# The opening of a decoder-layer kernel: x first, the modulation of feature block 0 alone, and four idle-fill products

## The reference, cut to what matters

```
mod = silu(c) @ w_ada + b_ada          # w_ada 1024 x 6144; six rows of 1024: sh1 sc1 gt1 sh2 sc2 gt2
h   = rms_norm(x, g_norm_mix) * (1 + sc1) + sh1
proj = h @ w_in                        # columns: q f i g | attention q k v | merge gates
```

## Time and profile before

| what | value |
|---|---|
| median of three runs | 951.63 us |
| profiled execution | 952.29 us |
| its span, first to last instruction | 950.6 us |
| TensorE busy | 915.2 us (96%) |
| VectorE, ScalarE, GpSimd busy | 441.2, 363.2, 439.2 us |
| mean granted TensorE clock, of full | 0.995 |
| HBM read | 111.76 MB |

### The profile page before, as it was taken

One profiled execution on the slowest core, in us unless ns is written; L12 is line 12 of the kernel. 1 busy time (PEld: TensorE's weight loads), 2 busy tenths in 40 slices (PEclk: granted clock), 3 DMA queues, 4 the chain that ended last, 5 costly groups with the idle time before them and its releaser, 6 DMA issues.

```text
span 950.6 us, 11767 instructions
## 1 busy us (share of the span) xinstructions
PE 915.2 (96%) x4487; PEld 771.1 (81%) x4487; DVE 441.2 (46%) x707; ACT 363.2 (38%) x482; POOL 439.2 (46%) x390
## 2 busy tenths in 40 slices
PE   2999999998999999999999999999999999999996
PEld 1788888987888888888888888888888888888885
DVE  4843467765456979976723526232222222200005
ACT  4433425242344223453323326555444544412113
POOL 2588433443243344345544445644544445444554
PEclk9999999999999999999999999999999999999998
DMA  9832221212143758443435131322223322233212
GB/s 316 264 132 89 89 89 45 89 45 89 45 142 132 225 175 287 147 133 123 189 104 214 60 132 45 128 95 88 88 88 99 120 89 88 88 122 100 89 44 89
DMA packets 93767, 114.47 MB, mean 120 GB/s; under 512 B 2158, under 2 KB 84250, under 8 KB 93726
## 3 DMA queue, kind: packets, MB, share of 16 engines
q1 hardware_dynamic: 93726, 113.89, 36.1%
HBM read 111.76 MB, written 2.12 MB: 120 GB/s over the span
## 4 chain that ended last, share of the span: by engine, by line
PE 44%; issue 30%; POOL 19%; DVE 3%; ACT 1%; DMA 1%; POOLq 0%; SPq 0%; DVEq 0%; ACTq 0%
PE bank L1051 44%; POOL w_lo L656 18%; DVE bank L1514 1%; DMA x_in<-in_x_dram 1%; DVE bank L1988 0%; DVE x L1989 0%; PE bank L1054 0%; DVE xn_ffn L1885 0%; ACT h_tmp L762 0%; POOL masks L593 0%; ACT w_hi L735 0%; POOL masks L630 0%; DVE h_tmp2a L1570 0%; DVE part L1516 0%; DVE bank L1512 0%
## 5 line engine op out<-in xcount | busy, mean ns | idle before, releaser
L656 POOL TENSOR_TENSOR w_lo<-w_raw,w_hi 128x512 fp32r<-128x512 f32 x292 | 387.3, 1357 | 457.5 <-ACT w_hi L735 452.5
L1051 PE MATMUL bank<-h_hi,w_hi 128*128 128x512 f32 (+1 forms) x880 | 340.3, 390 | 0.1
L1051 PE MATMUL bank<-h_lo,w_hi 128*128 128x512 f32 (+1 forms) x880 | 336.7, 386 | 0.0
L1051 PE MATMUL bank<-h_hi,w_lo 128*128 128x512 f32 (+1 forms) x880 | 261.1, 385 | 0.0
L735 ACT ACTIVATE w_hi<-w_raw 128x2048 fp32r<-128x2048 f32 x72 | 137.5, 1910 | 223.2 <-PE bank L1051 223.2
L1051 PEld LDWEIGHTS bank<-h_hi,w_lo 128*128 128x128 f32 x880 | 165.6, 188 | 33.2
L1051 PEld LDWEIGHTS bank<-h_lo,w_hi 128*128 128x128 f32 x880 | 165.4, 188 | 32.8
L1051 PEld LDWEIGHTS bank<-h_hi,w_hi 128*128 128x128 f32 x880 | 165.1, 188 | 32.8 <-POOL h_lo L643 0.3
L1051 PE MATMUL bank<-w_hi,act_hi 128*128 128x512 f32 x176 | 68.5, 389 | 0.0
L1051 PE MATMUL bank<-w_lo,act_hi 128*128 128x512 f32 x176 | 68.5, 389 | 0.0
L1051 PE MATMUL bank<-w_hi,act_lo 128*128 128x512 f32 x176 | 68.5, 389 | 0.0
(11 more groups left out here) (250 smaller groups left out, 1133.6 us busy)
## 6 DMA issues: line engine op xcount, KB each, us to landing
w_raw<-in_w_in_dram SPq DMA_DIRECT2D x32, 1024.0 KB, 5.2
w_raw<-in_w_up_dram SPq DMA_DIRECT2D x22, 1024.0 KB, 5.0
ada<-in_w_ada_dram SPq DMA_DIRECT2D x16, 1024.0 KB, 5.3
w_raw<-in_w_down_dram SPq DMA_DIRECT2D x11, 1024.0 KB, 4.8
ada<-in_w_ada_dram SPq DMA_DIRECT2D x16, 512.0 KB, 8.4
w_raw<-in_w_out_dram SPq DMA_DIRECT2D x4, 1024.0 KB, 5.1
x_in<-in_x_dram SPq DMA_DIRECT2D x4, 512.0 KB, 5.4
w_raw<-in_w_in_dram SPq DMA_DIRECT2D x8, 256.0 KB, 7.2
```

The source lines that it names most:

```text
L656: ins = pool.tensor_tensor(wlo[slot][:, cols], raw[slot][:, cols], whi[slot][:, cols].bitcast(F32), ALU.subtract)
L1051: return pe.matmul(o, lhsT, rhs, start=start, stop=stop, **kw)
```

## The change

The four feature pairs become five groups, `MOD_GROUPS`: block 0 alone, block 1 alone, then pairs. A single block's modulation is a sum over 256 columns, two products with ones, and so on. The loads of w_ada come in quarters of the 1024 rows, two DMAs each (128 columns of shift and of scale per row for a single block, 256 for a pair), so there are 40 issues in place of 16; the shares of pair 0 follow the first group and the other shares follow the groups of pairs 1 to 3. The seven loads of small rows are issued by ScalarE at its start.

Each tile of x gets its own inverse root on GpSimd; VectorE scales tiles 0 to 2 and ScalarE tile 3. TensorE first transposes the small rows, then block 0 and 1 of each tile as it comes, with a product of 512 columns that nothing reads behind each of tiles 0, 1 and 2 (`full_rate`: the identity with the normed x, into a bank that unit 0 later starts anew), and one of 256 columns behind the first modulation. VectorE makes a group's sums and then its `modulated`, in strict turn. All low parts of h but those of blocks 6 and 7 are GpSimd's, now ahead of the shares. ScalarE makes h of a pair ahead of its shares' conversion, and a unit's share waits for its own load alone. TensorE runs a pair's products by pass over both units: high with high, the next blocks' transposes, high with low h, the next modulation, low weights. SyncE's unit 2 waits for the third group's modulation, and VectorE's conversion of it for the fourth's and the last shares' high parts. The remaining hunks rename semaphore counts.

```diff
+MOD_GROUPS = ((0,), (1,), (2, 3), (4, 5), (6, 7))
...
+        def group_columns(g):
+            k0, n = MOD_GROUPS[g][0], len(MOD_GROUPS[g]) * P
+            return ada[k0 // 2][:, :, 256 * (k0 % 2):256 * (k0 % 2) + 2 * n]
...
+            def ada_quarter(g, q):
+                ks = slice(2 * q, 2 * q + 2)
+                k0, n = MOD_GROUPS[g][0], len(MOD_GROUPS[g]) * P
+                for i in range(2):
+                    sp.dma_start(group_columns(g)[:, ks, n * i:n * i + n],
+                                 cols_of(w_ada, D * i + P * k0, n)[:, ks, :]).then_inc(ada_in[g][q], 16)
+            def first_shares(j):
+                for u in range(2):
+                    sp.dma_start(raw[u][:, 512 * j:512 * j + 512].rearrange("p (k c) -> p k c", c=256),
...
+            for g in range(len(MOD_GROUPS)):
+                for q in range(4):
+                    ada_quarter(g, q)
+                if g != 1:
+                    first_shares(max(g - 1, 0))
+            ready(sp, ("mod1", 2))
             sp.dma_start(raw[2][:, :].rearrange("p (k c) -> p k c", c=256), unit_source(2)).then_inc(raw_in[0], 16)
...
-            pool.wait_ge(sq_done, TT)
-            inverse_root(0, TT)
+            for t in range(TT):
+                pool.wait_ge(sq_done, t + 1)
+                link(pool.tensor_scalar(rstd[:, t:t + 1], ssq[:, t:t + 1], 1.0 / D, EPS, ALU.mult, ALU.add))
+                pool.tensor_tensor(rstd[:, t:t + 1], rstd[:, t:t + 1], mhalf[:, 0:1], ALU.pow).then_inc(first_root, 1)
...
             for j in range(KT // 2):
+                if j < KT // 2 - 1:
+                    low_h(2 * j)
+                    if j:
+                        low_h(2 * j + 1)
                 low_share(j, 0)
                 low_share(j, 1)
-                if 0 < j < KT // 2 - 1:
-                    low_h(2 * j)
-                if j < KT // 2 - 1:
-                    low_h(2 * j + 1)
+                if j == 0:
+                    low_h(1)
...
+            def rows(dst, r0, src, n):
+                act.dma_start(dst[r0:r0 + n, :], src).then_inc(vec_in, 16)
+            rows(vec_rows, B_ADA, b_ada.rearrange("l (k p) -> (l k) p", p=P), 48)
...
             def high_share(j, u):
                 cols = slice(512 * j, 512 * j + 512)
+                act.wait_ge(share_in[j][u], 16)
...
-            act.wait_ge(rstd_done, 1)
-            for t in range(TT - 1):
-                act.activation(xn_in[:, t, :], x_in[:, t, :], ACT.Copy, scale=rstd[:, t:t + 1]).then_inc(xn_done[0], 1)
+            t = TT - 1
+            act.wait_ge(first_root, TT)
+            act.activation(xn_in[:, t, :], x_in[:, t, :], ACT.Copy, scale=rstd[:, t:t + 1]).then_inc(xn_done[t], 1)
             for j in range(KT // 2):
-                act.wait_ge(share_in[j], 16 * 2)
-                high_share(j, 0)
+                if j == 0:
+                    high_share(j, 0)
+                first_h(2 * j)
+                if j:
+                    first_h(2 * j + 1)
+                    high_share(j, 0)
                 high_share(j, 1)
-                first_h(j)
                 if j == 0:
+                    first_h(1)
                     act.wait_ge(lbd_done, 1)
...
+            def first_modulation(g):
+                b = claim(pe, ("mod1", g))
+                pe.wait_ge(pair_done, g + 1)
+                for t in range(2 * len(MOD_GROUPS[g])):
+                    ins = mm(b[:, t:t + 1], part[:, g % 2, t * P:(t + 1) * P], ones[:, 0:1])
+                filled(ins, ("mod1", g))
+            def full_rate(t, n):
+                mm(bank[BANKS["g", 0, 0][0]][:, 0:n], ident[:, :], xn_in[:, t, 0:n])
             def transposed_x(k):
                 b = claim(pe, ("xT", 0, k))
-                if k == 0:
-                    pe.wait_ge(xn_done[0], TT - 1)
-                    pe.wait_ge(xn_done[1], 1)
                 for t in range(TT):
                     ins = transpose(b[:, t * P:(t + 1) * P], xn_in[:, t, k * P:(k + 1) * P])
                 filled(ins, ("xT", 0, k))
+            def first_transposes():
+                bb = [claim(pe, ("xT", 0, k)) for k in range(2)]
+                for t in range(TT):
+                    pe.wait_ge(xn_done[t], 1)
+                    for k in range(2):
+                        ins = transpose(bb[k][:, t * P:(t + 1) * P], xn_in[:, t, k * P:(k + 1) * P])
+                        if t == TT - 1:
+                            filled(ins, ("xT", 0, k))
+                    if t < TT - 1:
+                        full_rate(t, S)
...
+            def growing_products(u, k, w, a):
+                j = k // 2
+                hi, lo = (s[u][:, :].rearrange("p (k c) -> p k c", c=256) for s in (whi, wlo))
+                if w is wlo:
+                    if j < KT // 2 - 1:
+                        pe.wait_ge(lo_share, 2 * j + u + 1)
+                    else:
+                        pe.wait_ge(lo_done, u + 1)
+                elif a is h_lo:
+                    pe.wait_ge(h_lo_done[k], 1)
                 else:
                     pe.wait_ge(h_hi_done, k + 1)
+                    if j < KT // 2 - 1:
+                        pe.wait_ge(hi_share, 2 * j + u + 1)
+                    else:
+                        pe.wait_ge(hi_done, u + 1)
...
+            high, h_low, w_low = (whi, h_hi), (whi, h_lo), (wlo, h_hi)
+            vector_rows()
+            first_transposes()
+            first_modulation(0)
+            full_rate(3, 256)
+            for u in range(2):
+                growing_products(u, 0, *high)
+            first_modulation(1)
+            for u in range(2):
+                growing_products(u, 0, *h_low)
+            for u in range(2):
+                growing_products(u, 0, *w_low)
+            for u in range(2):
+                growing_products(u, 1, *high)
+            for k in (2, 3):
                 transposed_x(k)
-            vector_rows()
-            for j in range(KT // 2):
-                first_modulation(j)
-                if j:
-                    growing_products(j - 1, 1)
-                if j < KT // 2 - 1:
-                    for k in (2 * j + 2, 2 * j + 3):
-                        transposed_x(k)
-                growing_products(j, 0)
-            growing_products(KT // 2 - 1, 1)
+            for what in (h_low, w_low):
+                for u in range(2):
+                    growing_products(u, 1, *what)
+            first_modulation(2)
+            for g in (2, 3):
+                for k in MOD_GROUPS[g]:
+                    for u in range(2):
+                        growing_products(u, k, *high)
+                for k in MOD_GROUPS[g + 1]:
+                    transposed_x(k)
+                for k in MOD_GROUPS[g]:
+                    for u in range(2):
+                        growing_products(u, k, *h_low)
+                first_modulation(g + 1)
+                for u in range(2):
+                    for k in MOD_GROUPS[g]:
+                        growing_products(u, k, *w_low)
+            for u in range(2):
+                for what in (high, h_low, w_low):
+                    for k in MOD_GROUPS[-1]:
+                        growing_products(u, k, *what)
             for u in range(U_UP):
...
+            def group_sums(g):
+                n = 2 * len(MOD_GROUPS[g]) * P
+                acc = bank[6][:, 0:n]
+                if g:
+                    dve.wait_ge(pair_done, g)
+                if g >= 2:
+                    ready(dve, ("mod1", g - 2))
                 for k in range(KT):
-                    if k % 4 == 0:
-                        dve.wait_ge(ada_in[j][k // 4], 16 * 2)
+                    if k % 2 == 0:
+                        dve.wait_ge(ada_in[g][k // 2], 16 * 2)
...
-                    if j == 1 and k == 1:
-                        low_h(0)
-                    if j > 1 and k == 1:
-                        modulated(j - 1)
...
+            def scaled_x(t):
+                dve.wait_ge(first_root, t + 1)
+                dve.wait_ge(x_in_s[t], 16)
+                ts(xn_in[:, t, :], x_in[:, t, :], rstd[:, t:t + 1], None, ALU.mult).then_inc(xn_done[t], 1)
+            scaled_x(0)
+            b = ready(dve, "vec")
+            link(dve.tensor_copy(vec[:, :], b[:, 0:N_VEC]))
+            release(dve.tensor_copy(convc[:, :], b[:, N_VEC:N_VEC + 88]), "vec")
+            tt(lbd[:, :], vec[:, LB:LB + 4], vec[:, LB + 4:LB + 8], ALU.subtract).then_inc(lbd_done, 1)
+            for t in range(1, TT - 1):
+                scaled_x(t)
+            for g in range(len(MOD_GROUPS)):
+                group_sums(g)
+                modulated(g)
             for k in (KT - 2, KT - 1):
```

More of the change, by code:

```diff
@@ L345, in layer_kernel @@
         hi_done = sem("hi_done")
-        share_in = [sem(f"share_in{j}") for j in range(KT // 2)]
+        share_in = [[sem(f"share_in{j}_{u}") for u in range(2)] for j in range(KT // 2)]
         hi_share, lo_share = sem("hi_share"), sem("lo_share")
@@ L353, in layer_kernel @@
         c_in, vec_in = sem("c_in"), sem("vec_in")
```

(28 more changed lines are left out.)

140 lines of the change are left out of this document (35 added, 105 removed).

## The result

| kernel | median us | lowest to highest | unit 2's first product |
|---|---|---|---|
| before | 952.25 (4 runs) | 951.01 to 952.90 | 53.81 |
| after | 963.17 (4 runs) | 962.48 to 963.84 | 64.26 |

The ratio is 1.0116, interval 1.0099 to 1.0134. The 951.63 that the forecast was added to is the median of three of the four runs of before. The profiled span grew from 950.6 to 961.0, by 10.4, and unit 2's first product moved by 10.45. The shift is complete there; in this pair of executions nothing is lost or won after it. The side, the place and the order of events were forecast; the size was more than double, and lies outside the range.

A forecast was written before the change was run, and what follows sets the result against it. The prediction took VectorE's modulation sums to bound the opening's first third and TensorE the rest. Its opening sum of +4.1 us plus 0.8 for the clock was rounded to +5.0, 956.6 us, with its own range 954.4 to 958.6.

The forecast's parts named there:

- The sum of a cycle: Opening, scale to next scale of a pair: TensorE, waiting for shares converted behind the blocks, takes 9.75 us, twice.
- VectorE's 7.85: Opening, one pair's cycle if VectorE alone set it: sums 6.3, modulation 1.1, small operations 0.43, 7.85 us in all.
- Rival (1): Opening cycles: conversions do not pace them, VectorE's 7.85 does; unit 2 at 53.2, -0.6 us (951.0); chance 0.08.
- rival (4): Opening not decisive: shift partly soaked up in waits between 60 and 300 us, or early start worth more; +0.5 to +2; chance 0.08.
- rival (5): Opening: the early start survives whole, needing conversions not to pace and cheaper split sums; -2 us or more; chance 0.03.
- the sum: Opening up to unit 2's first product: steps added up put it at 57.95 against 53.81 before, +4.1 us.
- last blocks to unit 2: End of the opening: 3.35 us for share 0, then twenty-four products, 5.46, until unit 2 can start at 57.95.
- The clock term: TensorE behind the new 4 us wait ahead of block 2: lower clock costs 0 to 1.7 us, 0.8 taken.
- rival (3): TensorE in the opening: every one of three waits is followed by the slow clock, 1.7 each; +9.2 us; chance 0.06.
- rows that land late: Small-row loads on ScalarE's queue: landing after 10, they would make TensorE hold every transpose; no reason seen for it.
- a lock on block 1's scale: VectorE's last small operation for block 1, beside GpSimd's work: 0.8 us added, putting the scale at 21.8.
- Rival (2): Weight loads of blocks 0 and 1: 512-byte pieces move at half rate; +4.6 us on the sum, +9 in all; chance 0.05.

The follow-up runs named there:

- experiment 1: Changed kernel with both weight shares of pairs 1 to 3 converted ahead of their feature blocks on ScalarE, as before: 957.64 us, ratio 1.0053.
- experiment 11: experiment 1 with the next modulation ahead of the low products, additions left as the change has them: 954.71 us, ratio 1.0024.
- Experiment 5: experiment 1 plus additions inside the next group's sums and the next modulation ahead of the low products: 952.71 us, ratio 1.0002.
- 9: Experiment 5 with modulation 2 ahead of block 1's low-weight products and the small rows' transposes and copies behind x: 951.37 us, ratio 0.9996.
- 12: 9 with five more fill products that nothing reads, all in early waits: 951.13 us, ratio 0.9992.
- experiment 2: Changed kernel, order kept, with eleven more products that nothing reads in TensorE's waits: 959.75 us, ratio 1.0076.
- 4: Changed kernel without its own four idle-fill products: 962.89 us, ratio 1.0108.
- 8: Changed kernel with blocks 0 and 1 as one group of 512 columns again: 963.26 us, ratio 1.0113.
- experiment 6: Experiment 5 with idle-fill products in the waits: 952.57 us, ratio 1.0004.
- experiment 10: Kernel before with only ScalarE's new order, blocks ahead of share conversions for pairs 1 to 3, and the wait it needs: 963.82 us, ratio 1.0122.
- experiment 3: Changed kernel with shares converted ahead of the blocks and the waits filled (three, one and one products ahead of the pairs): 956.21 us, ratio 1.0040.

## Why the prediction was wrong

**The ladder.** By medians: after 963.2; shares ahead of the blocks 957.6; modulation ahead of the low products 954.7; additions inside the next group's sums 952.7; modulation 2 earlier and the rows later 951.4; waits filled 951.1. The first three rungs are the new order of issue on ScalarE, TensorE and VectorE; together they are 10.5 of the 10.9. The rungs are not free of the clock: from 29 us to the end of the opening the low clock lasted 10.3 us in after, 6.8 in experiment 1, 3.4 in each of experiments 11 and 5, and 0 in 9 and 12. So the 10.5 is the price of the orders with the slow stretches that came with them.

**What held.** The mechanism: TensorE paced the cycle through shares converted behind the blocks, in three waits, 4.0, 2.3 and 2.3 forecast, 3.93, 1.96 and 1.96 seen. The sum of a cycle: 9.75, and 9.57 at full clock in experiment 2. VectorE's 7.85, seen as 7.9 in experiment 11. The shift at unit 2 is the shift at the end, within 0.1. Rival (1) is refuted by 11.95 and 11.09, rival (4) by the equal shifts, rival (5) by the result.

**What failed.** Unit 2 moved by 10.45, the sum said 4.1; the 6.3 between lie like this ("scale" is the end of a block's last small operation):

| stretch | forecast | measured | excess |
|---|---|---|---|
| to scale 0 | 16.35 | 17.58 | 1.23 |
| to scale 1 | 5.45 | 5.66 | 0.21 |
| to scale 2/3 | 7.85 | 8.09 | 0.24 |
| first cycle | 9.75 | 11.95 | 2.20 |
| second cycle | 9.75 | 11.09 | 1.34 |
| last blocks to unit 2 | 8.80 | 9.89 | 1.09 |

*The clock term, taken at 0.8.* The prediction priced one slow stretch at 1.7 and took about half of that; the waits of the second cycle and the end it priced at nothing. In the two cycles the eight high products took 3.55 and 3.46, against 2.0 in the sum and 1.99 at full clock in experiment 2: 3.0 more. The first cycle's transposes took 1.56 from their start to the next product's, the second's 0.82 at full clock: 0.7 more. So the clock cost about 3.8 in the two cycles where 0.8 was counted. Their excess over the sum is 3.5, not 3.8, since other terms partly cancel: the sum's 1.2 for two transposed blocks was too high (it had read 0.6 off a row's whole passage), the way from a scale to the first high product was 3.47 for 3.3 in both, and the low products 0.1 to 0.2 longer. A few tenths more lie in modulation 1, 0.99 for 0.6, and in modulation 2, which began 0.45 behind its sums. Experiment 2 gave back 3.4 with one slow stretch left. It is the largest of the mis-sized terms, and rival (3), held at 0.06, is nearest to what happened: its +9.2 stands 1.7 under the result. It was not exactly that rival: one of its three waits was followed by the full clock, and another slow stretch stood before it, at the first product. What spoke against it, "TensorE is busy for most of each cycle", was a guess about the gate from an average. The trace had only one case of a long wait behind the opening, and that one had been followed by a slow stretch. By the Trainium skill (TensorE: Matmul & The Clock Gate, HAM oscillation) a kernel whose bursts of products stood between waits of some 3 to 5 us paid a slow stretch each time. The wait of 3.93 here agrees; of the two of 1.96, shorter than the page's, one was followed by a slow stretch and one was not. 0.8 was the wrong end to lean to.

*A step that was missing: the bank behind the last products.* VectorE converts unit 2's weight, and in the change it may do so only behind ScalarE's last share. That wait is short, 0.4. What costs more is the company: GpSimd, whose last two shares also come behind ScalarE's now, subtracts from 57.76 on, and beside it the conversion takes 1.84 and its neighbour `oml` 1.25 for four columns. Before, GpSimd was idle then:

```profile
49.55 1.22 DVE L1561 CAST w_hi<-w_raw 128x2048 fp32r<-128x2048 f32 x1
50.69 0.16 DVE L1563 TENSOR_SCALAR oml<-lb 128x4 f32<-128x4 f32 x1
```

Then a memset of 1.76 stands between them and `hq`, which frees bank 0. TensorE had ended block 7's products and waited: its last twenty-four products would have let unit 2 start near 63.3, and it started at 64.26. The prediction followed the last products on TensorE only, and never asked which engine had to free the bank behind them: 1.0 of the 1.1 us in the last row. The wait is there in experiments 2, 4 and 8 as well (0.7 to 0.8 in their rows). In experiment 1, with the shares ahead, the two operations take 1.22 and 0.16 and the wait is absent.

*Prices of the early part.* The sums began at 12.25 for 11.7, since the small rows landed only at 9.8, TensorE transposes them first, and VectorE copies them out before it scales tile 1; the prediction had named rows that land late as a danger and seen no reason for it. A step of 256 columns repeats every 0.52, not 0.445: 490 ns against the 412 of the nearest row, eight steps in 4.15 for 3.6, twice. Against it, the 0.8 of a lock on block 1's scale did not occur (0.16). Together +1.7 at scale 2/3.

*Rival (2), half rate for the 512-byte pieces*, is refuted on this path: the stretches with block 1's pieces, the first with a part of the shares in it, ran at 304 to 322 GB/s, and no sum waited for them.

```profile
13.00:16.00 3.00, 2.06 (x8) 0.84 (x6) 2.79 (x7) 1.56 (x2) 0.00 (x0) 1.00 1.18 304
16.00:19.00 3.00, 1.12 (x6) 0.74 (x6) 2.13 (x7) 1.36 (x3) 0.00 (x0) 1.00 1.15 322
```

**What stays open.** Experiment 5 has all three orders as before and an early start, and is not faster. Part of it is shown (modulation 2 behind products, then the DMA at 36). Experiment 12 loses 0.8 of its 2.0 us at unit 2 in the longer slow stretch at 220; why that stretch was 6.8 us long there and in experiment 6, and 3.4 in 5 and 9, wasn't settled, and its median is inside what can be told from no change. Each kernel was profiled in one execution, so how much the stretches vary between executions of one kernel is not known either. Which idle and which work decide whether a slow stretch follows a wait was not isolated: three waits of nearly 2 to 4 us had different outcomes, and in experiment 2 a stretch came with no wait over 0.9 ahead of it.

## What to carry to other kernels

When an order of issue is changed, write down for each engine what stands ahead of the first instruction that the next engine waits for, conversions and frees of banks too: 6 us of gained start were worth nothing, and three reorderings of work that was the same in amount cost 10.5, slow stretches included. If a change opens new waits on TensorE, price the work behind each at the lower clock as the main case, where the trace has one such wait with a slow stretch behind it. And test a reordering first in the old kernel alone (experiment 10): one small edit showed a loss as large as the whole, if partly through other waits.

## What the runs showed of the hardware that was not expected

- Eleven products that nothing reads made a kernel 3.4 us faster, eight of them placed in the three waits of 2 to 4 us. The four of the change itself, all placed before 17.7 us, did nothing to the time that can be measured. But three such products in experiment 3, caught by a slow stretch, ran 2.0 past the wait that they were to fill.
- The granted clock reads 1.00 from the start of the old kernel, where its modulation 0 took 1.84 for 0.95 later: the column can't be trusted there, the spacing of the products can.
- A multiply-add of 256 columns on a PSUM bank took 490 ns where an operation of another kind took 412; halving the columns saved 35% and not half.
- The last of seven loads of 2 to 33 KB, issued on ScalarE's queue between 0.8 and 3.6 us, landed only at 9.8, behind three of the four tiles of x that SyncE's queue had issued from 1.3 (the third was used from 8.63, the fourth from 10.07): another queue did not carry it past them.
- A small VectorE operation beside a GpSimd subtraction took 1.25 (128x4) and 1.32 us (the last scale of experiment 1) where 0.16 is its time alone, and a cast of 2048 columns 1.84 for 1.22.
